# Attention values with a ones column, output scaling on VectorE, and five re-placed steps

## The reference

```
s = einsum('bhqd,bhkd->bhqk', qb, kh) + cb[..., :, None] - c[:, :, None, :]
s = where(kpos <= qpos, s, -inf)
o = einsum('bhqk,bhkd->bhqd', softmax(s), vh)
```

## Time and profile before

| | us |
|---|---|
| median of 3 runs (4329.23 to 4346.8) | 4336.57 |
| the profiled execution | 4341.13 |
| its span | 4339.4 |

### The profile page before, as it was taken

One profiled execution on the slowest core, in us unless ns is written; L12 is line 12 of the kernel. 1 busy time (PEld: TensorE's weight loads), 2 busy tenths in 40 slices (PEclk: granted clock), 3 DMA queues, 4 the chain that ended last, 5 costly groups with the idle time before them and its releaser, 6 DMA issues.

```text
span 4339.4 us, 74155 instructions
## 1 busy us (share of the span) xinstructions
PE 4182.0 (96%) x21298; PEld 3645.9 (84%) x21298; DVE 2963.0 (68%) x5277; ACT 1759.9 (41%) x3256; POOL 2821.3 (65%) x1651
## 2 busy tenths in 40 slices
PE   8999999999999999999999999989999999999998
PEld 6787877789999997888877878878899999988887
DVE  6745434467788767898966544344677877688888
ACT  3155022124677653333331540221246776533333
POOL 6854864765577666666668548657556776666665
PEclk9999999999999999999999999999999999999999
DMA  3233954825699998999822339448256999989997
GB/s 106 91 112 112 287 154 146 246 79 156 226 344 363 315 309 305 350 340 346 290 78 92 117 107 297 149 144 240 78 165 244 343 354 321 296 311 341 349 346 277
DMA packets 494909, 1011.83 MB, mean 233 GB/s; under 512 B 51536, under 2 KB 320464, under 8 KB 491856
## 3 DMA queue, kind: packets, MB, share of 16 engines
q1 hardware_dynamic: 420656, 739.77, 52.9%
q0 software_dynamic: 73728, 268.47, 17.3%
q10 hardware_dynamic: 288, 1.05, 0.1%
HBM read 846.57 MB, written 162.53 MB: 233 GB/s over the span
## 4 chain that ended last, share of the span: by engine, by line
PE 80%; DMA 7%; DVE 4%; issue 4%; SPq 2%; ACT 2%; POOL 1%; DVEq 0%; another core or an unknown queue 0%; ACTq 0%; POOLq 0%
PE bank L1363 14%; PE pair L1024 7%; PE bank L1367 7%; PE bank L1024 6%; PE sums L1415 5%; PE sums L1420 5%; PE sums L1425 5%; PE pair L1026 4%; PE sums L1394 3%; PE bank L1026 3%; DMA ring<-v_tab 3%; PE bank L1415 2%; PE bank L1093 2%; PE bank L1425 2%; PE bank L1420 2%
## 5 line engine op out<-in xcount | busy, mean ns | idle before, releaser
L863 POOL TENSOR_TENSOR w_hi<-ring,ones 128x1024 fp32r<-128x1024 f32 x272 | 540.1, 1986 | 588.2 <-PE bank L1050 177.2
L1363 PE MATMUL bank<-xT,w_hi 128*128 128x384 f32 x2048 | 709.8, 347 | 6.4 <-ACT w_hi L1831 3.4
L866 POOL TENSOR_TENSOR w_lo<-ring,w_hi 128x1024 fp32r<-128x1024 f32 x272 | 686.2, 2523 | 21.3
L1363 PE MATMUL bank<-xl_peer,w_hi 128*128 128x384 f32 x2048 | 689.0, 336 | 0.0
L850 POOL TENSOR_TENSOR w_lo<-ring,w_hi 128x1024 fp32r<-128x1024 f32 x192 | 463.0, 2412 | 304.3 <-ACT w_hi L1831 298.0
L857 POOL TENSOR_TENSOR cl<-att,ch 128x384 fp32r<-128x384 f32 x256 | 377.8, 1476 | 332.4 <-ACT ch L1906 330.9
L1837 ACT CAST w_hi<-ring 128x1024 fp32r<-128x1024 f32 x252 | 266.0, 1055 | 671.7 <-PE bank L1425 496.3
L2729 DVE TENSOR_TENSOR w_lo<-ring,w_hi 128x1024 fp32r<-128x1024 f32 x252 | 338.3, 1342 | 121.0 <-ACT w_hi L1837 119.0
L1367 PE MATMUL bank<-xT,w_lo 128*128 128x384 f32 x2048 | 396.9, 334 | 0.0
L1363 PEld LDWEIGHTS bank<-xT,w_hi 128*128 128x128 f32 x2048 | 388.5, 190 | 7.9 <-issue 3.9
L1363 PEld LDWEIGHTS bank<-xl_peer,w_hi 128*128 128x128 f32 x2048 | 388.3, 190 | 0.0
(11 more groups left out here) (418 smaller groups left out, 9859.3 us busy)
## 6 DMA issues: line engine op xcount, KB each, us to landing
ring<-v_tab SPq DMA_DIRECT2D x252, 512.0 KB
ring<-w_stream SPq DMA_DIRECT2D x240, 512.0 KB
g_spill<-gst SPq DMA_DIRECT2D x240, 192.0 KB
vg<-w_spill SPq DMA_DIRECT2D x64, 704.0 KB
att<-u_tab SPq DMA_DIRECT2D x320, 128.0 KB, 4.5
u_turned<-att SPq DMA_DIRECT2D x80, 512.0 KB, 5.2
ring<-u_tab SPq DMA_DIRECT2D x256, 128.0 KB
ring<-u_turned SPq DMA_DIRECT2D x64, 512.0 KB
```

The lines of the kernel that those rows point to most:

```text
L863: nc.gpsimd.tensor_tensor(w_hi[b][:, 0:n], src, ones[:, 0:1].to_broadcast([P, n]), ALU.mult)\
L866: nc.gpsimd.tensor_tensor(w_lo[b][:, 0:n], src, w_hi[b][:, 0:n].bitcast(F32), ALU.subtract)\
L1363: nc.tensor.matmul(out, w_hi[s % 2][:, c * P:(c + 1) * P], dense_parts(c)[part], start=(c == 0 and part == 0), stop=False)
```

## The change

The value tile gets, per head, 64 values and two columns of ones (width 66). Step V multiplies 65 columns, so the row sum comes out beside the output. The mask is a third product in step S: an identity times the mask, held in the first two slots of `sel`, which POOL fills. DVE loses the mask addition and gains the scaling of the output, and ACT loses both the scaling and the row sum. DVE's loop now follows the list of steps: at S the maximum, then, where there is one, the turn; at V the reciprocal and the scaling. Step Y comes later in the list.

```diff
@@ fox_steps
         if k < 16:
             seq.append(("S", k))
-        if k > 16 and more:
-            seq.append(("S", k - 1))
+        if k == 17 and more:
+            seq.append(("S", 16))
+        if k == 11:
+            seq.append(("Y", 0))
         if k >= 3:
             seq.append(("V", k - 3))
-            if (k - 3) % 8 == 7:
-                seq.append(("Y", (k - 3) // 8))
+    if more:
+        seq.append(("S", 17))
+    seq.append(("Y", 1))
@@ fox_scores (PE)
                     for a in range(2):
                         nc.tensor.matmul(..., start=(a == 0), stop=False)
+                    nc.tensor.matmul(bank[b][:, t * P:(t + 1) * P], sel[:, 0, :], sel[:, 1, :], start=False, stop=True)\
+                        .then_inc(filled[b].sem, 1)
@@ step V (PE)
-                                mm = nc.tensor.matmul(bank[7][:, 0:FOX_D], pT[...], v_sb[...], ...)
+                                mm = nc.tensor.matmul(bank[7][:, 0:FOX_D + 1], pT[...], v_fox[:, kb, 4 * i + h, 0:FOX_D + 1], ...)
@@ ACT, attention
-                                         bias=nmax[:, e:e + 1], accum_out=rsum[:, e:e + 1])\
+                                         bias=nmax[:, e:e + 1])\
                         if kind == "V":
-                            ...
-                            nc.scalar.activation(ytok[...], bank[7][:, 0:FOX_D], ACT.Copy, scale=rinv[:, u:u + 1])\
-                                .then_inc(drained_sem[7], 1)
                             n7 += 1
@@ DVE, attention (new)
+                def over_row_sum(c, i, u, n7):
+                    at = FOX_D * (u // 4 % 2)
+                    dve.wait_ge(filled[7].sem, filled[7].at(L, "FQ", i, n7 + 1))
+                    c.step(V.reciprocal(rinv[:, u:u + 1], bank[7][:, FOX_D:FOX_D + 1]))
+                    c.wait()
+                    V.tensor_scalar(ytok[:, u % 4, at:at + FOX_D], bank[7][:, 0:FOX_D], rinv[:, u:u + 1], None, ALU.mult)\
+                        .then_inc(drained_sem[7], 1)
+                def maxima_and_outputs(i, first=False, last=False):
+                    for kind, u in fox_steps(not last):
+                        if kind == "S":
+                            row_maximum(i + u // 16, u % 16)
+                            if u == 5 and not first:
+                                low_part(L, "FQ", i - 1, y_lo, yT, y_hi, 2)
+                            if u in (2, 3):
+                                fox_key_low(i, 3, u - 2)
+                            ...
+                            if u in (7, 11, 15) and not last or u == 3 and not first:
+                                turn_single(L, "FQ", i if u > 3 else i - 1, u // 4 - 1 if u > 3 else 3)
+                        if kind == "V":
+                            over_row_sum(c, i, u, n7)
+                        if kind in "VY":
+                            n7 += 1
@@ POOL, ahead of FZ
+                nc.gpsimd.tensor_copy(sel[:, 0, :], ident[:, :]).then_inc(sel_ready.sem, 1)
+                nc.gpsimd.tensor_copy(sel[:, 1, :], mask_q[:, :]).then_inc(sel_ready.sem, 1)
@@ ACT, LRU stage
                 lru_high(L, 0)
-                values(L, "FV", 0)
                 decay_tanh(1)
                 decay_exp(1)
+                values(L, "FV", 0)
                 decay_root(1)
@@ PE, last_heads: slot by slot instead of both slots chunk by chunk
-                    for s in range(2):
+                        pe.wait_ge(y_lo_ready.sem, y_lo_ready.at(L, "MQ", 3, 1))
                         terms(s, (KC - 2,))
-                    pe.wait_ge(y7_lo_ready.sem, y7_lo_ready.at(L, "MQ", 0, 1))
-                    for s in range(2):
+                        pe.wait_ge(y7_lo_ready.sem, y7_lo_ready.at(L, "MQ", 0, 1))
                         terms(s, (KC - 1,)).then_inc(proj_done, 1)
@@ DVE, heads (MQ)
-                    turn_single(L, "MQ", i, 1)
                     decay_mask(i + 1, 1)
                     gated(i, 1)
+                    turn_single(L, "MQ", i, 1)
+                    weigh(i + 1, 0)
                     turn_single(L, "MQ", i, 2)
-                    weigh(i + 1, 0)
                     weigh(i + 1, 1)
@@ DVE, last_heads
                     normalise(c, 3, 0)
-                    low_part(L, "MQ", 0, ...)
                     normalise(c, 3, 1)
-                    low_part(L, "MQ", 1, ...)
                     gated(3, 0)
+                    low_part(L, "MQ", 0, ...)
-                    low_part(L, "MQ", 2, ...)
                     gated(3, 1)
+                    for i in (1, 2): low_part(L, "MQ", i, ...)
@@ DVE, OUT: the last two of the turns of MC stand behind take_out(0, t)
@@ DVE, experts: turn(24) and turn(25) stand ahead of the first one-hot rows
```

More of the change, by code:

```diff
@@ L124 @@
 VW = P + 2
-VPAD = TT * ML_H * (VW - P)
+FW = FOX_D + 2
+VPAD = TT * FOX_H * (FW - FOX_D)
 class Count:
@@ L307, in build @@
         ytok = att[:, 4096:4608].rearrange("p (t n) -> p t n", t=TT)
-        nmax, rsum, rinv = (floor[:, 0, 16 * n:16 * n + 16] for n in range(3))
+        nmax, rinv = (floor[:, 0, 16 * n:16 * n + 16] for n in range(2))
         E = att[:, 0:4096].rearrange("p (a s n) -> p a s n", a=2, s=4)
@@ L1169, in fox_scores @@
                     for a in range(2):
[L1170 to L1172 removed]
+                        nc.tensor.matmul(bank[b][:, 0:(t + 1) * P], fox_q[pp][hp][:, a, t * P:(t + 1) * P],
+                                         fox_k[pp][hp][:, a, 0:(t + 1) * P], start=(a == 0), stop=False)
+                    nc.tensor.matmul(bank[b][:, t * P:(t + 1) * P], sel[:, 0, :], sel[:, 1, :], start=False, stop=True)\
+                        .then_inc(filled[b].sem, 1)
                 for s in range(4):
@@ L1518, in values @@
                 for t in range(TT):
-                    nc.scalar.copy(v_sb[:, t, i * SEQ:(i + 1) * SEQ], bank[t][:, :]).then_inc(drained_sem[t], 1)
+                    nc.scalar.copy(v_fox[:, t, 8 * i:8 * i + 8, 0:FOX_D], bank[t][:, :].rearrange("p (h d) -> p h d", d=FOX_D))\
+                        .then_inc(drained_sem[t], 1)
             def lru_high(L, i):
@@ L1671, in _ @@
                     n7 = 0
-                    todo = []
                     for kind, u in fox_steps(i < 3):
@@ L2244, in _ @@
                     fox_key_low(0, 1, hp)
-                def scores_and_roots(i, first=False, last=False):
-                    c = Chain(dve, dve_step, L, "FQ", i)
[L2248 to L2270, removed]
@@ new lines, in row_maximum @@
+                def row_maximum(i, u):
+                    b, n = 4 + u % 2, (u % 4 + 1) * P
+                    dve.wait_ge(filled[b].sem, filled[b].at(L, "FQ", i, u // 2 + 1))
+                    V.tensor_reduce(nmax[:, u:u + 1], bank[b][:, 0:n], AX.X, ALU.max, negate=True)\
+                        .then_inc(srow_ready.sem, 1)
+                def over_row_sum(c, i, u, n7):
[5 more added lines that the diff above has]
+                        .then_inc(drained_sem[7], 1)
@@ new lines, in maxima_and_outputs @@
+                def maxima_and_outputs(i, first=False, last=False):
+                    c = Chain(dve, dve_step, L, "FQ", i)
+                    n7 = 0
+                    for kind, u in fox_steps(not last):
[5 more added lines that the diff above has]
+                                fox_key_low(i, 3, u - 2)
+                            if u in (10, 11) and not last:
+                                fox_query_low(i + 1, 0, u - 10)
+                            if u in (12, 13) and not last:
+                                fox_key_low(i + 1, 1, u - 12)
+                            if u in (7, 11, 15) and not last or u == 3 and not first:
[4 more added lines that the diff above has]
+                            n7 += 1
+                    c.close()
@@ L2273, in scores_and_roots @@
                             fox_query_low(i + 1, 2, hp)
-                    c.close()
                 for hp in range(2):
                     fox_query_low(0, 2, hp)
-                scores_and_roots(0, first=True)
+                row_maximum(0, 0)
+                row_maximum(0, 1)
+                maxima_and_outputs(0, first=True)
                 with dve.Fori(1, 3) as i:
-                    scores_and_roots(i)
-                scores_and_roots(3, last=True)
+                    maxima_and_outputs(i)
+                maxima_and_outputs(3, last=True)
                 low_part(L, "FQ", 3, y_lo, yT, y_hi, 2)
@@ L2381, in last_heads @@
                     normalise(c, 3, 0)
+                    normalise(c, 3, 1)
+                    gated(3, 0)
                     low_part(L, "MQ", 0, y_lo, yT, y_hi, 1)
[L2383 to L2386, removed]
                     gated(3, 1)
+                    for i in (1, 2):
+                        low_part(L, "MQ", i, y_lo, yT, y_hi, 1)
                     c.close()
@@ L2426, in _ @@
                     merge_turning(L, "MC", i, 4 * i + (AHEAD_AT["MC"] - 4))
-                for n in range(AHEAD - 4, AHEAD):
+                for n in range(AHEAD - 4, AHEAD - 2):
```

(7 more changed lines are left out.)

26 lines of the change are left out of this document (10 added, 16 removed).

## The result

The changed kernel takes 4405.65 us (median of 4 runs, 4398.1 to 4414.5), the kernel before 4333.44 us beside it (4 runs): ratio 1.0159, 95% interval 1.0135 to 1.0183. It is slower by 72 us; the prediction said 4395 and 59.

What follows compares the result with a forecast made beforehand. The prediction took PE, busy 96% of the span, as the bound. Its terms, 66 + 5 + 33 - 45 = +59 us, took the profiled 4341.1 to 4400, as a median 4395; range 4350 to 4438.

Steps and rivals of the forecast that it cites:

- The step that decides: Attention: outputs on DVE stand behind the turn's DMA wait, stopping TensorE at V5, V9, V13, V1; +66 us.
- The stop and the clock: Attention: longer intervals between ring loads +66 us; lower granted clock behind 22 stops +33, bounds 0 and 73.
- The rival on the faster side: Attention: outputs never hold TensorE since the block has landed when DVE comes to its turn; 4277 us, chance 0.07.
- The outputs' own work: Attention, DVE: reciprocal 0.15 us and scaling 0.22, with starts and waits 0.5; bounds 0.4 and 0.6.
- TensorE hardly notices: Attention before the change: DVE's wait for its block barely delays TensorE, as T8 is due only about then.
- the signs: Expected trace of the attention stage: about 22 waits of 3 to 4 us, stage 40 to 50 us longer a layer.
- The other edits: MQ, last_heads, OUT, experts and TensorE's slot order: each removes a PE wait; together -45 us, bounds 30 and 54.
- MQ and last_heads: DVE's order: `weigh` ahead of the turn, 5.7 us a layer; `gated(3, 0)` ahead of two low parts, 3.8.
- TensorE slot by slot and OUT: Slot 0 finished first: 4.2 us a layer plus 3.3 of clock; two turns behind `take_out(0)`: 2.2.
- The experts' 11.4: Experts stage: turn(25) ahead of the one-hot rows saves 3.9 us a layer, plus 1.8 of clock.
- Without the clock: Attention: same stops, but TensorE is rarely throttled; 4362 us, chance 0.16.
- Every stop cold: Attention: the low clock follows every stop, 73 us instead of 33; 4435 us, chance 0.12.

Runs made afterwards that it cites:

- the block there in time: Changed kernel with SP issuing the store of the last block and the next block's four loads ahead of the ring load, DVE's order untouched: 4316.5 us, ratio 0.9951.
- the stops cut to ten of 1.9 us on average: Changed kernel with 14 unread 128x128 products on TensorE ahead of each V that stops behind a turn: 4405.0 us, ratio 1.0169.

## Why the prediction was right, and where it was not

- **The step that decides held.** DVE's turn holds the output, the output holds bank 7, and TensorE stops at V instead of at T. Shown from two sides: with the turn behind V6, and with the block there in time, TensorE's stops in layer 0 go from 34.9 to 0.6 and 7.1 us, and 112 and 89 us come back.
- **The stop and the clock: right in sum, shared out wrongly.** I had 66 and 33, together 99; the ring loads show 101.3. Windows from ring load to ring load put 43 us of this down to the low clock and leave 58 for the stop. At the full clock the intervals of blocks 0 and 1 are 14.1 to 14.5 us, for the 14.3 of the sum, and those of block 3, less the time that the low clock takes, are 13.6 to 14.7. Those of block 2 are 17.5 to 20.9 us, all six with the low clock in them (0.71 to 0.90); less its time they are 14.9 to 15.8, for 15.9. The term that was too long is the one from ring issue to turn: 7.9 taken, 7.65 measured on average, which over 22 intervals is 6 us. So the stop was sized 8 too high and the clock 10 too low, and that their sum came within 3 us is luck. The stops themselves were not all of the 3.3 to 4.3 us of the prediction: 16 of the 24 are 2.8 to 4.3, and the six at V9 and the first of each layer 1.5 to 1.8.
- **A slip.** Between the ring loads at 256.86 and 397.40 lie twelve intervals, not eleven. The sum counted twelve (eight, three and one) and is not touched. The rival on the faster side divided by eleven: 140.5 / 12 = 11.7 us against 10.9 leaves 24 x 0.8 = 19 us, not 42. The late turn on the kernel before gave 19 too.
- **The outputs' own work.** The scaling took 0.28 us for the 0.22 taken, a reciprocal and a scaling 0.5 with their gap. Within its bounds, and without weight.
- **TensorE hardly notices: wrong.** The late turn on the kernel before shows that DVE's wait cost it 19 us. The statement is not in the sum of the forecast, which starts from the measured 140.5 and 143.4.
- **What lies outside the intervals.** 107.6 - 101.3 = 6 us, for the 5 of the mask products and Y0. The stage is 54.8 and 52.8 us longer a layer, where the signs had said 40 to 50 although the sum held 52.
- **The other edits: -45, measured -43.2.** MQ and last_heads are 20 us alone (19 predicted). TensorE slot by slot and OUT are 8.8 + 8.0 by the stage table, for 2 x 9.7. The experts' 11.4 did not come. By runs and stages I can name 37; the other 6 are as large as what two such medians leave open. The LRU move, taken at 0, has no run of its own.
- **The rivals.** Without the clock 4362: against it stand the windows, 0.92 and 0.91 over the stage. Every stop cold 4435: behind the stops at 319, 333, 398 and 412 us the clock stayed at 1.00, and 42 us are far from 73. The Trainium skill, "TensorE: Matmul & The Clock Gate", section "HAM oscillation — how this bites in real kernels", says of a loop with long enough DMA waits that every pass starts cold. This case's trace agrees for the longest stops: the clock fell behind each of the five of 3.5 to 4.0 us in layer 0. Of the other seven there, 1.5 to 3.3 us long, it fell behind three. The faster side, 4277: its condition is met with the turn behind V6, and that kernel takes 4294. So the side exists, and its price was 17 us too good. Even so the outputs on DVE gain nothing over the outputs on ACT: 0.9909 against 0.9897 for the other edits with the old attention, and 0.9876 with its turn late.
- **The 11 us that the prediction was short** are the attention's 111.6 against 104, the others' 43.2 against 45, and 1 that these differences of medians leave over.

## What to carry to other kernels

An instruction that waits for a DMA belongs where nothing behind it in its engine's queue is wanted soon. Before work is moved onto another engine, list what that engine's queue waits for, and count how many steps of the busiest engine lie between the wait and the first step that needs what stands behind it: here one place in DVE's order was worth 86 us, with the same instructions. The kernel before had such a wait too, and moving its turn two units later gave 19 us without any other edit. A wait that starts with the busiest engine's own progress (a slot ends, a load is issued, a block lands, a turn, an output, the next slot) is a loop, and it is the loop's length that counts, not the length of the wait in it.

## What was not expected of the hardware

- A 128x128 product has a record of 0.22 us where it stands between others (at 406.42 us of the changed kernel) and takes 0.12 us in a row of fourteen. Price by the distance of starts, not by the record.
- The granted clock does not follow the length of a stop alone: 0.50 for 12 us behind 3.97 us of idle time and 1.00 behind 3.26 (333.67), but 0.64 over the 9 us behind another of 3.26 (2585.29, in layer 1). With the stops cut to ten of 1.9 us on average it still fell behind some, and with no stop above 1.3 us (the turn one place later) it was 1.00 in one layer and 0.97 in the other. What makes it fall is open.
